# The first half of an output projection moved into the SSD chunks, on x rows kept on chip, with decay rows read by broadcast

## The chip, the cores and the metric

The kernel runs on one core of one Trainium2 chip. The metric is the device time of one execution, in microseconds (us), median of three runs. The engines are TensorE (PE, with its weight loads PEld), VectorE (DVE), ScalarE (ACT), GpSimd (POOL) and the DMA queues, which SyncE (SP) and GpSimd feed. Each engine runs its own stream of instructions in order; streams meet at semaphores.

## What is computed

Two transformer-like blocks, sequence 1024, width 1024, float32. The change is in the second one:

```python
h = rmsnorm_2(x, norm1_w); p = h @ w_in
y_ssd = ssd_mixer(...)     # Mamba-2, 8 chunks of 128 tokens, 16 heads of 64, 2 groups, state 128
y_ml  = mlstm_mixer(...)   # 8 heads of 128
x = x + concat([y_ssd, y_ml]) @ w_out          # (1024 x 2048) @ (2048 x 1024)
x = x + hier_moe(rmsnorm_2(x, norm2_w)); return rmsnorm_2(x, norm_f_w)

# one SSD chunk, per head
a_cs = cumsum(dt*a);  L = exp(a_cs[l] - a_cs[s]) for s <= l, else 0
y = (C B^T * L) @ (dt*x) + (C @ state) * exp(a_cs)
state = state * exp(a_cs[-1]) + B^T @ (exp(a_cs[-1]-a_cs) * dt*x)
y = group_rmsnorm((y + D*x) * silu(z)) * norm_w
```

## The kernel before

The program is a row of stages, each a block that all engines leave together. In the second block they are `projections`, `ssd_chunks`, `mlstm_chunks` and `second_block`, then the routed experts.

**Products in high and low halves.** Every large product takes three float32r products (`mm3`, L343 to L345): high x high, high x low, low x high. Each operand is split into a high half (ACT copy to float32r) and a low half (DVE subtraction). `h_hl` (called `hl` in the code) is the one big buffer with both halves of a 1024 x 1024 activation.

**`ssd_chunks`** loops over 8 chunks. The carried state binds them: chunk k+1's `inter` product (C times state, L1758) needs chunk k's new state. Per chunk, PE does: `inter`; `intra` (16 small products of the masked matrix `sd_l` with dt*x, L1767); `state` (L1773); then `front(k+1)`, which makes the sums over the chunk (L1720), C B^T (L1722), turns x and B (L1727, L1731) and builds the exponents of L for 16 heads in PSUM: four broadcast products of `adt` with a triangle (L1737) and one of the identity with a matrix of -1e30 (L1739) for each four heads, in a PSUM pair `sd_psA` that they share with the transposes; last `result(k)`, which turns y (L1747). ACT copies x, squares y, takes the root, and takes the 16 exponentials of `sd_l` (L1613) in two halves (`decay`), the first before and the second after the root. DVE adds and scales y, carries the state (L1680, L1683), makes dt*x and its decayed copy (L1648, L1650), multiplies `sd_l` by C B^T (L1656) and writes the turned y times its gain to `sd_yt` (L1702). GpSimd only makes D*x (L1564); ahead of the loop its queue writes 15 blocks of zeros to `scratch_ys` (L1558). The turned y goes to DRAM (`scratch_y_ssd`, L1539).

**`second_block`** has three stages after `mlstm_chunks`, which leaves its own result in `h_hl`: `add_product` "w1" (`h_hl` times the lower half of w_out, added to x rows that a DMA brings, L799), `load_split` "ys" (y_ssd read back and split into `h_hl`), and `add_product` "w2" with the upper half of w_out and the following norm ("n4"). An `add_product` loads 16 weight tiles of 128x512 (L791), splits them (ACT L809, DVE L823), and runs 16 sums of 24 products.

## Time and profile before

| | us |
|---|---|
| median of 3 runs (3782.6 to 3791.38) | 3783.6 |
| the profiled execution | 3789.3 |
| its span | 3787.6 |
| stage `ssd_chunks`, 2401.6 to 2581.2 | 179.6 |
| stage `mlstm_chunks`, 2581.2 to 2825.4 | 244.2 |
| stage "w1", 2825.4 to 2931.9 | 106.5 |
| stage "ys", 2931.9 to 2949.5 | 17.6 |
| stage "w2" with its norm, 2949.5 to 3062.5 | 113.0 |

The times of the stages are positions in the profiled execution, counted from the start of its span. The profiled execution is 0.15% above the median of the runs. A busy share of an engine is that of the whole stage; what a stage costs is read from its ends, since no engine works across them.

### The profile page before, as it was taken

Reading aid. Unit: us, or ns where it says so; the run is one execution under the profiler, and the core shown is the slowest. Engines: PE = TensorE matmul, PEld = TensorE weight load, DVE = VectorE, ACT = ScalarE, POOL = GpSimd, SP = SyncE. Lnnn points to the kernel's source line nnn. Section 1 sums busy time; section 2 is a strip of 40 time slices with the busy share of each in tenths; the row PEclk is TensorE's granted clock in tenths of the full one; section 3 lists DMA queues with packets and bytes.
Section 4 is the critical chain, followed back from the end, with each engine's and each line's share of the span. In section 5 each row is a group of like instructions: output and inputs, shape, how many; then the busy total and the mean of one; then the engine's idle time right before and its main releaser. Section 6 shows DMA issues by size and latency. Waiting matters only on the chain. (4 is left out here: it accounts for less than half of the span.)

```text
span 3787.6 us, 40241 instructions
## 1 busy us (share of the span) xinstructions
PE 3401.2 (90%) x15444; PEld 2779.5 (73%) x15444; DVE 1902.0 (50%) x2156; ACT 1371.0 (36%) x1950; POOL 217.9 (6%) x309
## 2 busy tenths in 40 slices
PE   6999999898899999996999999787969759999994
PEld 5888888686788888885887788666857647777773
DVE  3444433433344554446206553473431468888885
ACT  4322333212311111113312322343550327878783
POOL 0000000000000000000010000210000110000002
PEclk8999999998999999998999999896769879999997
DMA  3122221432111111112232223422121329999996
GB/s 96 62 73 91 66 76 58 161 111 100 45 50 50 50 38 45 50 39 72 98 83 67 95 95 106 167 78 95 67 82 43 114 97 362 393 386 391 388 387 235
DMA packets 325203, 489.17 MB, mean 129 GB/s; under 512 B 58848, under 2 KB 223200, under 8 KB 324064
## 3 DMA queue, kind: packets, MB, share of 16 engines
q1 hardware_dynamic: 292496, 372.25, 28.8%
q0 software_dynamic: 27984, 98.58, 6.9%
q10 hardware_dynamic: 4608, 16.78, 1.1%
q8 instruction: 75, 1.23, 0.1%
q14 instruction: 40, 0.33, 0.0%
HBM read 402.08 MB, written 85.46 MB: 129 GB/s over the span
## 5 line engine op out<-in xcount | busy, mean ns | idle before, releaser
L947 DVE TENSOR_TENSOR x_rows<-x_rows,ff_psd 128x512 f32<-128x512 f32 x352 | 239.5, 688 | 333.8 <-PE ff_psd L345 333.8
L343 PE MATMUL m_ps<-h_hl,m_w_hl 128*128 128x512 f32 x896 | 356.0, 397 | 11.6 <-DVE m_w_hl L530 11.6
L344 PE MATMUL m_ps<-h_hl,m_w_hl 128*128 128x512 f32 x896 | 349.4, 390 | 0.0
L345 PE MATMUL m_ps<-h_hl,m_w_hl 128*128 128x512 f32 x896 | 349.4, 390 | 0.0
L2415 DVE TENSOR_TENSOR h_hl<-ex_stage,h_hl 128x1024 fp32r<-128x1024 f32 x256 | 304.8, 1221 | 39.5 <-ACT h_hl L2411 38.2
L2411 ACT ACTIVATE h_hl<-ex_stage 128x1024 fp32r<-128x1024 f32 x256 | 269.1, 1058 | 81.2 <-DMA ex_stage<-in_exp_w_up_dram 46.6
L343 PE MATMUL pj_turned<-h_hl,pc_w_hl 128*128 128x512 f32 x576 | 224.9, 390 | 6.2 <-DVE pc_w_hl L1290 6.2
L344 PE MATMUL pj_turned<-h_hl,pc_w_hl 128*128 128x512 f32 x576 | 224.2, 389 | 0.0
L345 PE MATMUL pj_turned<-h_hl,pc_w_hl 128*128 128x512 f32 x576 | 224.1, 389 | 0.0
L343 PEld LDWEIGHTS m_ps<-h_hl,m_w_hl 128*128 128x128 f32 x896 | 168.6, 188 | 50.5 <-DVE m_w_hl L530 12.0
L927 ACT ACTIVATE ff_act_hl<-ff_act 128x1024 fp32r<-128x1024 f32 x22 | 23.3, 1060 | 485.4 <-DVE ff_act L965 485.4
L344 PEld LDWEIGHTS m_ps<-h_hl,m_w_hl 128*128 128x128 f32 x896 | 168.6, 188 | 38.6 <-issue 3.8
L345 PEld LDWEIGHTS m_ps<-h_hl,m_w_hl 128*128 128x128 f32 x896 | 168.5, 188 | 35.2
L2415 DVE TENSOR_TENSOR ex_w_hl<-ex_stage,ex_w_hl 128x1024 fp32r<-128x1024 f32 x128 | 154.0, 1222 | 47.6 <-ACT ex_w_hl L2411 46.6
L530 DVE TENSOR_TENSOR m_w_hl<-m_stage,m_w_hl 128x1024 fp32r<-128x1024 f32 x56 | 68.5, 1223 | 193.6 <-ACT m_w_hl L458 193.6
L343 PE MATMUL ff_psg<-h_hl,ff_wg 128*128 128x512 f32 x352 | 139.5, 396 | 22.3 <-DVE ff_wg L938 11.3
L2411 ACT ACTIVATE ex_w_hl<-ex_stage 128x1024 fp32r<-128x1024 f32 x128 | 133.0, 1056 | 56.3 <-DMA ex_stage<-in_exp_w_gate_dram 47.2
L343 PE MATMUL ff_psd<-ff_wd,ff_act_hl 128*128 128x512 f32 x352 | 137.7, 391 | 4.3 <-DVE ff_act_hl L967 4.3
L343 PE MATMUL w_ps<-w_w_hl,h_hl 128*128 128x512 f32 x256 | 105.7, 413 | 39.2 <-DVE w_w_hl L823 39.2
L344 PE MATMUL ff_psd<-ff_wd,ff_act_hl 128*128 128x512 f32 x352 | 137.6, 391 | 0.0
L344 PE MATMUL ff_psg<-h_hl,ff_wg 128*128 128x512 f32 x352 | 137.6, 391 | 0.0
L345 PE MATMUL ff_psg<-h_hl,ff_wg 128*128 128x512 f32 x352 | 137.5, 391 | 0.0
(498 smaller groups left out, 7751.3 us busy)
## 6 DMA issues: line engine op xcount, KB each, us to landing
ex_stage<-in_exp_w_gate_dram SPq DMA_DIRECT2D x128, 512.0 KB, 5.4
ex_stage<-in_exp_w_up_dram SPq DMA_DIRECT2D x128, 512.0 KB, 7.6
ex_stage<-in_exp_w_down_dram SPq DMA_DIRECT2D x128, 512.0 KB, 6.3
m_stage<-in_w_in_dram SPq DMA_DIRECT2D x56, 512.0 KB, 4.1
...
```

Source lines behind the costliest of these rows:

```text
L343: nc.tensor.matmul(out, w_hl[0], x_hl[0], start=first, stop=False)
L344: nc.tensor.matmul(out, w_hl[0], x_hl[1], start=False, stop=False)
L345: return nc.tensor.matmul(out, w_hl[1], x_hl[0], start=False, stop=last)
L530: v.tensor_tensor(w_hl[s][:, 1], stage[:, s], f32(w_hl[s][:, 0]), ALU.subtract).then_inc(s_lo, 1)
L927: nc.scalar.activation(a_hl[b][:, 0], act_f[:], ACT.Copy).then_inc(s_ah, 1)
L947: v.tensor_tensor(dst, dst, ps_d[g % NB][:], ALU.add).then_inc(s_add, 1)
L2411: nc.scalar.activation(w_hl[u][:, 0], stage[:, s], ACT.Copy).then_inc(s_hi, 1)
L2415: nc.vector.tensor_tensor(w_hl[u][:, 1], stage[:, slot(e, u)], f32(w_hl[u][:, 0]), ALU.subtract).then_inc(s_lo, 1)
```

## The change

One. `ssd_chunks` no longer builds the exponents of L on PE. The running sums of `adt` are made once, as 16 rows, by PE and DVE in `projections` and stored to a new DRAM tensor `scratch_cum`. In `ssd_chunks` a DMA reads the 16 rows of a chunk into all 128 partitions (`sd_cum_l`, 1 MB, one buffer). GpSimd adds the mask (`causal`, a 128x2048 addition) into `sd_l`, which now has two buffers. ACT takes the exponentials from there. Sums over chunks are made once for all 8 chunks, ahead of the loop.

Two. C B^T is copied to SBUF (`sd_cb`, new `c_by_b`), and the product with `sd_l` reads it there. The decay of the state moves from DVE to GpSimd.

Three. The 15 stores of zeros move to the end of `projections`, on SP's queue, from a 128x128 tile.

Four. The x rows (`x_rows3`, 4 MB) are loaded at the start of `ssd_chunks` and stay. The upper half of w_out is loaded and split there into `h_hl`, which is free until `mlstm_chunks`: eight tiles ahead of the loop, eight in its first pass (`w_high`, `w_low`). The turned y of a chunk is split (`sd_y_hl`), and `out_product(k-1)`, 48 products of 128x512, stands between `front(k+1)` and `result(k)` on PE. DVE adds it to the x rows (`add`).

Five. The store of y, the stage "ys" and one of the two `add_product` stages are gone. The one that is left keeps the norm and loads no x rows.

```diff
@@ projections, engine SP, behind the loads of the column weights
+            sp.wait_ge(s_zero, 1)
+            for x in range(scr.NX):
+                row = (scr.NT - 2 * T + x) * P
+                sp.dma_start(scr.ys[row:row + P, :].rearrange("p (a n) -> p a n", n=P),
+                             zero[:].unsqueeze(1).to_broadcast([P, KT, P])).then_inc(s_zst, 16)
+            sp.wait_ge(s_zst, 16 * scr.NX)
...
@@ projections, engine PE
+                elif f == 9:
+                    pe.wait_ge(s_up, 2)
+                    pe.wait_ge(s_rows, 1)
+                    for k in range(T):
+                        last = nc.tensor.matmul(ps_cum[:, k * P:(k + 1) * P], scr.adt[:, k], upper[:], start=True, stop=True)
+                    last.then_inc(s_pcum, 1)
...
@@ ssd_chunks, engine SP
                 sp.dma_start(xbc[:, k % 2], scr.xbc[k]).then_inc(s_xbc[k % 2], 16)
+                if k >= 1:
+                    sp.wait_ge(g_l, k)
+                sp.dma_start(cum_l[:].rearrange("p h n -> p (h n)"),
+                             scr.cum[k].rearrange("(a h) n -> a (h n)", a=1).broadcast_to([P, H * P])).then_inc(s_cum, 16)
...
             chunk_loads(1)
-            for k in range(NC):
-                if k + 2 < NC:
-                    chunk_loads(k + 2)
-                sp.wait_ge(d_yt, 2 * k + 2)
-                sp.dma_start(scr.y_ssd[:, :, k * P:(k + 1) * P].rearrange("f p s -> p f s"), yt[:]).then_inc(s_st, 16)
-            sp.wait_ge(s_st, 16 * NC)
+            for n in range(NW):
+                h, k = divmod(n, XT)
+                wait(sp, s_wlo, n - NS + 1)
+                sp.dma_start(stage[:, n % NS], w_v[:, k, h * HALF:(h + 1) * HALF]).then_inc(s_w[n % NS], 16)
+            for k in range(2, NC):
+                chunk_loads(k)
@@ ssd_chunks, engine POOL
+            pool.dma_start(x_tm[:], scr.x4.rearrange("(t p) d -> p t d", p=P)).then_inc(s_x, 16)
+
+            def causal(k):
+                pool.wait_ge(s_cum, 16 * (k + 1))
+                wait(pool, p_in, k - 1)
+                nc.gpsimd.tensor_tensor(lt[:, k % 2], cum_l[:], neg[:].unsqueeze(1).to_broadcast([P, H, P]),
+                                        ALU.add).then_inc(g_l, 1)
...
             for k in range(NC):
-                pool.wait_ge(a_A, 6 * k + 2)
                 if k:
-                    pool.wait_ge(d_y, k)
-                nc.gpsimd.tensor_tensor(heads(xd[:]), heads(x_r[:]), per_head(d_row[:]), ALU.mult).then_inc(g_x, 1)
-            pool.wait_ge(s_zst, 16 * scr.NX)
+                    pool.wait_ge(p_inter, k)
+                    pool.wait_ge(d_st, k)
+                    nc.gpsimd.tensor_tensor(heads(state[:]), heads(state[:]), per_head(e3[:, 2, k]), ALU.mult).then_inc(g_st, 1)
+                if k + 1 < NC:
+                    skip(k + 1)
+                if k + 2 < NC:
+                    causal(k + 2)
@@ ssd_chunks, engine ACT
+            def decay(k, g):
+                act.wait_ge(g_l, k + 1)
+                for h in range(g * HG, (g + 1) * HG):
+                    last = nc.scalar.activation(lt[:, k % 2, h], lt[:, k % 2, h], ACT.Exp, bias=ncum[:, k, h:h + 1])
+                last.then_inc(a_l, 1)
...
+            decay(0, 0)
+            decay(0, 1)
+            for n in range(XT):
+                w_high(n)
             for k in range(NC):
                 if k + 1 < NC:
                     front(k + 1)
+                    decay(k + 1, 0)
                 act.wait_ge(d_y, k + 1)
...
                 if k + 1 < NC:
-                    decay(k + 1, (2, 3))
+                    decay(k + 1, 1)
+                if k == 0:
+                    for n in range(XT, NW):
+                        w_high(n)
+                act.wait_ge(d_yt, 2 * k + 2)
+                wait(act, p_w2, 2 * k)
+                nc.scalar.activation(yh[:, 0], yt[:], ACT.Copy).then_inc(a_yh, 1)
@@ ssd_chunks, engine PE
+            def out_product(k):
+                pe.wait_ge(d_yl, k + 1)
+                for h in range(2):
+                    cut = slice(h * HALF, (h + 1) * HALF)
+                    if k == 0:
+                        pe.wait_ge(s_wlo, XT * (h + 1))
+                    wait(pe, d_add, 2 * (k - 1) + h + 1)
+                    for t in range(XT):
+                        last = mm3(nc, psD[:, h], (yh[:, 0, t], yh[:, 1, t]), (hl[:, 0, t, cut], hl[:, 1, t, cut]),
+                                   t == 0, t == XT - 1)
+                    last.then_inc(p_w2, 1)
...
                 if k + 1 < NC:
                     front(k + 1)
+                    c_times_b(k + 1)
+                if k:
+                    out_product(k - 1)
                 result(k)
+            out_product(NC - 1)
@@ program
-            x_tm = second_block(nc, A, scr.x4, scr, hl, ctx)
-            routed_experts(nc, A, scr, hl)
+        recycle_semaphores(nc)
+        add_product(nc, "w1", x_tm, hl, A.w_out_2[0].rearrange("(k p) n -> p k n", p=P)[:, KT:],
+                    norm=("n4", A.norm2_w_2[0], dict(rows_out=scr.h)))
+        recycle_semaphores(nc)
+        routed_experts(nc, A, scr, hl)
```

The change writes the streams in another order. Three places show it; line numbers of the changed kernel differ from those before.

PE, one pass of the loop before, from the `state` product of one chunk to the `intra` products of the next:

```order
L1773 MATMUL sd_psC<-sd_xdec,sd_b 128x512 x2
L1720 MATMUL sd_psD<-adt,sd_upper 128x16
...
L1722 MATMUL sd_psD<-sd_xbc 128x128 x2
L1727 MATMUL sd_psA<-sd_ident,sd_xbc 128x128 x8
L1731 MATMUL sd_psE<-sd_ident,sd_xbc 128x128 x2
L1737 MATMUL sd_psA<-sd_upper,adt 128x128 x4
L1739 MATMUL sd_psA<-sd_neg,sd_ident_r 128x512
...
L1747 MATMUL sd_psA<-sd_ident,sd_y 128x128 x8
L1758 MATMUL sd_psC<-sd_state,sd_xbc 128x512 x2
L1767 MATMUL sd_psB<-sd_xdt,sd_l 128x64 x16
```

The same pass after (the rows of `mm3` stand 16 times each):

```order
L1854 MATMUL sd_psC<-sd_xdec,sd_b 128x512 x2
L1794 MATMUL sd_psA<-sd_ident,sd_xbc 128x128 x8
L1799 MATMUL sd_psA<-sd_ident,sd_xbc 128x128 x2
L1806 MATMUL sd_psB<-sd_xbc 128x128 x2
L343 MATMUL sd_psD<-h_hl,sd_y_hl 128x512
L344 MATMUL sd_psD<-h_hl,sd_y_hl 128x512
L345 MATMUL sd_psD<-h_hl,sd_y_hl 128x512
...
L1827 MATMUL sd_psA<-sd_ident,sd_y 128x128 x8
L1841 MATMUL sd_psC<-sd_state,sd_xbc 128x512 x2
L1847 MATMUL sd_psB<-sd_xdt,sd_l 128x64 x16
```

The 16 products and 4 mask products of the decay have left this place and the 48 products of the output have come in, ahead of the transposes of y.

DVE, one pass after, from the addition of the `intra` products on:

```order
L1731 TENSOR_TENSOR sd_y<-sd_y,sd_psB 128x1024
L1737 TENSOR_TENSOR sd_y<-sd_y,sd_xd 128x1024
L1739 TENSOR_TENSOR sd_y<-sd_y,sd_z 128x1024
L1743 TENSOR_TENSOR sd_state<-sd_state,sd_psC 128x1024
L1686 TENSOR_TENSOR sd_xdt<-sd_x,dt 128x1024
L1689 TENSOR_TENSOR sd_xdec<-sd_xdt,sd_e 128x1024
...
L1699 TENSOR_TENSOR sd_l<-sd_l,sd_cb 128x1024
L1713 TENSOR_TENSOR x_rows<-x_rows,sd_psD 128x512 x2
L1767 TENSOR_TENSOR sd_yt<-sd_psA,sd_norm 128x512 x2
L1770 TENSOR_TENSOR sd_y_hl<-sd_yt,sd_y_hl 128x1024
L1728 TENSOR_TENSOR sd_y<-sd_psC,sd_e 128x1024
```

Against before, the state's decay (L1680) is gone from it, and the copy of C B^T, two additions to the x rows and the low half of the turned y have come in, the additions ahead of `sd_yt`.

GpSimd, the end of its constants and its loop before:

```order
L1546 MEMSET sd_ones 128x128
L1547 MEMSET sd_eps 128x1
L1548 MEMSET sd_after 128x128
L1551 AFFINE_SELECT sd_after<-sd_after 128x128
L1554 MEMSET sd_zero 128x1024
L1558 DMA scratch_ys<-sd_zero 128x1024 x15
L1564 TENSOR_TENSOR sd_xd<-sd_x,sd_d 128x1024 x8
```

The same place after, to the first pass of the loop with a state to decay:

```order
L1594 DMA x_rows<-scratch_x 128x8x1024
L1599 TENSOR_TENSOR sd_l<-sd_cum_l,sd_neg 128x2048
L1605 TENSOR_TENSOR sd_xd<-sd_x,sd_d 128x1024
L1599 TENSOR_TENSOR sd_l<-sd_cum_l,sd_neg 128x2048
L1605 TENSOR_TENSOR sd_xd<-sd_x,sd_d 128x1024
L1599 TENSOR_TENSOR sd_l<-sd_cum_l,sd_neg 128x2048
L1616 TENSOR_TENSOR sd_state<-sd_state,sd_e 128x1024
```

Where GpSimd had one operation of 1024 columns a chunk it has two of them and one of 2048.

## Rows read from the trace of the kernel before

**Rows 1.** The page's first line.

```profile
span 3787.6 us, 40241 instructions
```

**Rows 2.** Busy time of each engine by stage, with the granted clock.

```profile
core 0: us, PE busy (x) PEld busy (x) DVE busy (x) ACT busy (x) POOL busy (x), PEclk, DMA share, GB/s
2825.40:2931.90 106.50, 96.14 (x384) 74.77 (x384) 21.59 (x32) 9.88 (x16) 0.96 (x1) 0.89 0.22 79
2931.90:2949.50 17.60, 0.00 (x0) 0.00 (x0) 9.82 (x9) 8.45 (x8) 0.00 (x0) 0.57 0.69 238
2949.50:3062.50 113.00, 99.08 (x448) 80.35 (x448) 48.83 (x55) 39.03 (x56) 19.84 (x11) 0.94 0.23 80
2401.60:2581.20 179.60, 136.86 (x828) 107.39 (x828) 117.28 (x118) 81.30 (x229) 28.60 (x34) 0.88 0.37 126
2581.20:2825.40 244.20, 200.46 (x1138) 185.17 (x1138) 85.47 (x189) 128.74 (x429) 16.57 (x26) 0.66 0.19 70
```

**Rows 3.** Timeline: the first instructions of the stages "w1" and "w2".

```profile
2825.44 9.02 SPq L791 DMA_DIRECT2D w_stage<-in_w_out_dram  x7
...
2949.53 9.65 SPq L791 DMA_DIRECT2D w_stage<-in_w_out_dram  x10
```

**Rows 4.** Who waits for whom, 2420 to 2575: total, times, longest.

```profile
PE sd_psA L1747 <- ACT sd_l L1613: 20.9, 14, 2.7
```

**Rows 5.** Timeline of one chunk: start, us, engine, line [idle before].

```profile
2504.89 1.22 DVE L1670 TENSOR_TENSOR sd_y<-sd_y,sd_psB 128x1024 f32<-128x1024 f32 x1 [2.36 <-PE sd_psB L1767]
...
2507.51 1.04 PE L1727 MATMUL sd_psA<-sd_ident,sd_xbc 128*128 128x128 f32 x8
...
2509.31 2.22 POOL L1564 TENSOR_TENSOR sd_xd<-sd_x,sd_d 128x1024 f32<-128x1024 f32 x1 [18.52 <-ACT sd_x L1599]
...
2509.80 1.22 DVE L1683 TENSOR_TENSOR sd_state<-sd_state,sd_psC 128x1024 f32<-128x1024 f32 x1
...
2510.94 1.67 DVE L1648 TENSOR_TENSOR sd_xdt<-sd_x,dt 128x1024 f32<-128x1024 f32 x1
...
2515.71 2.18 ACT L1613 ACTIVATE sd_l<-sd_psA,sd_neg_c 128x128 f32<-128x128 f32 x8
...
2518.85 3.10 PE L1758 MATMUL sd_psC<-sd_state,sd_xbc 128*128 128x512 f32 x4
...
2521.78 3.68 PE L1767 MATMUL sd_psB<-sd_xdt,sd_l 128*128 128x64 f32 x32
...
2525.30 1.94 PE L1773 MATMUL sd_psC<-sd_xdec,sd_b 128*128 128x512 f32 x4
...
2525.57 1.22 DVE L1670 TENSOR_TENSOR sd_y<-sd_y,sd_psB 128x1024 f32<-128x1024 f32 x1 [2.36 <-PE sd_psB L1767]
```

**Rows 6.** GpSimd's operation by tile: ns min/median/max, first and last start.

```profile
L1564 POOL TENSOR_TENSOR sd_xd<-sd_x,sd_d x8: 1896/2224/2598, 2413.1 to 2550.6; 128x1024 f32<-128x1024 f32 x8
```

**Rows 7.** As rows 2, five microseconds around an `inter` product.

```profile
2455.00:2460.00 5.00, 4.68 (x16) 2.46 (x15) 2.78 (x4) 0.67 (x3) 0.00 (x0) 0.66 0.19 53
```

**Rows 8.** Timeline of stage "w1": an addition for 24 products of 128x512.

```profile
2931.23 0.69 DVE L831 TENSOR_TENSOR x_rows<-x_rows,w_ps 128x512 f32<-128x512 f32 x1 [4.75 <-PE w_ps L345]
```

**Rows 9.** Timeline of `ssd_chunks`: first `intra` product, second chunk's addition of them.

```profile
2418.08 3.76 PE L1767 MATMUL sd_psB<-sd_xdt,sd_l 128*128 128x64 f32 x32 [0.85 <-DVE sd_l L1656]
...
2442.67 1.22 DVE L1670 TENSOR_TENSOR sd_y<-sd_y,sd_psB 128x1024 f32<-128x1024 f32 x1 [2.77 <-PE sd_psB L1767]
```

**Rows 10.** Weight tiles in stages "w1" and "w2", landing time of the x rows.

```profile
2841.66 0.63 ACT L809 ACTIVATE w_w_hl<-w_stage 128x512 fp32r<-128x512 f32 x1 [1.45 <-DMA w_stage<-in_w_out_dram]
...
2964.29 1.27 ACT L809 ACTIVATE w_w_hl<-w_stage 128x512 fp32r<-128x512 f32 x2 [1.06 <-DMA w_stage<-in_w_out_dram]
...
DMA to landing us min/median/max: 19.8/19.8/19.8
```

**Rows 11.** End of `projections`: column-weight loads; SP's queue, 2300 to 2402.

```profile
L1149 SPq DMA_DIRECT2D pc_stage<-in_w_in_dram x34: 367/368/678, 1981.5 to 2354.6; - x34
...
q1 hardware_dynamic: 6240, 3.15, 10.8%
```

402 lines of the change are left out of this document (199 added, 203 removed).

## The prediction

> **What bounds the kernel now.** I read the page first: the span is 3787.6 us [rows 1], against 3789.3 for the whole profiled execution and a median of 3783.6. Then one table by stage. The stages share nothing, so the change can be priced at three places: what goes, what `ssd_chunks` becomes, and what `projections` gets on top. `ssd_chunks` lasts 179.6 us and PE is busy 136.9 of them; "w1" lasts 106.5, "ys" 17.6 [rows 2]. Third I read the timeline of a chunk and the chain of waits. In a chunk nothing is saturated. The period is 20.68 us, from one addition of the `intra` products to the next (2504.89 to 2525.57) [rows 5]. It is a loop of short steps over three engines: y on DVE, square and root on ACT, the second half of the exponentials (2.18 us), the product with C B^T, the transposes, `inter`, `intra`, y again. The reader should see that PE stands still ahead of the transposes because `sd_psA` is held by exponents that ACT has not read: 20.9 us in 14 waits [rows 4]. Just behind that gap `inter` takes 3.10 us where `state`, four instructions of the same size, takes 1.94 [rows 5]; the granted clock of those five microseconds is 0.66 of 2.4 GHz, a mix of both levels [rows 7].
>
> **What goes.** From the first load of "w1" to the first load of "w2" are 2949.53 - 2825.44 = 124.1 us [rows 3]. The stage that is left is "w2" as it stood: same loads, products and norm, nothing else at its start. So **-124.1**, a difference of two positions and not an estimate. The store of y went with it.
>
> **What `projections` gets.** PE is the bound there, so its 8 products of 128 columns go on top: `state` does 8 pieces of 128 columns in 1.94 us [rows 5], so +1.9. The 15 stores of zeros (7.86 MB) start when the last column weights have been asked for, at 2354.6, and the stage ends at 2401.6. Loads in pieces of 512 bytes on SP's queue moved 3.15 MB in 10.8% of 102 us, 286 GB/s [rows 11]; 7.86 MB at that rate are 27.5 us, over at about 2382. I take 0. Cover gone (half the rate) it would end at 2410 and cost 8.
>
> **What a chunk becomes, on PE.** `inter` at full clock 1.94 (as `state`), `intra` 3.68, `state` 1.94. Ten transposes, two products for C B^T and eight transposes of y are 20 pieces of 0.13 (1.04 for eight) = 2.6, and 0.4 for ACT to empty `sd_psA` [rows 5]. The output product: in "w1" 24 products take 4.75 + 0.69 = 5.44 us [rows 8], so 48 take 10.9. Sum **21.4 us**, nearly without a gap, where a chunk had a period of 20.68. The decay's products are out of it, and so is the wait of rows 4, because ACT now reads SBUF.
>
> **On DVE.** Seven operations of 1024 columns from SBUF alone (add D*x, times z, dt*x, its decayed copy, two products with C B^T, low half of y), three from PSUM (the two y steps, state), each 1.22 [rows 5]: 12.2. The scale of y with the reciprocal about 1.0 (my estimate from half the columns), copy of C B^T 0.35, two additions to the x rows 2 x 0.69 [rows 8], `sd_yt` two halves 1.4 by the same row. Sum 16.3.
>
> **On GpSimd, and what it blocks.** `sd_xd` takes 1.90 at its shortest [rows 6]. One decay of state and one D*x are 3.8, the mask of 2048 columns by proportion another 3.8: 7.6 us a chunk against 1.9. Rows 5 show what this does to DVE. `sd_xd` runs from 2509.31 to 2511.53. `sd_xdt`, which reads SBUF only, starts at 2510.94 and takes 1.67 instead of 1.22, ending 1.08 behind GpSimd's end. `sd_state` with `sd_psC` starts at 2509.80, in the middle of it, and takes its usual 1.22. So an operation with a PSUM operand runs beside GpSimd, one from SBUF alone waits for its end. In the new order D*x falls where dt*x would start (both wait for the same x), and the mask falls on its decayed copy; the state's decay falls on the low half of y, ahead of the next y. The first two, 1.9 + 3.8 = 5.7, lie in a stretch in which DVE has no PSUM work of its own, so DVE and its blocked time come to 16.3 + 5.7 = **22.0 us**. The third is taken out of time in which DVE waits for PE anyway.
>
> The Trainium skill, "SBUF — State Buffer", section "SBUF: two separate sides", calls the pair of ports that DVE and GpSimd share an exclusive lock: whoever starts first keeps it for its whole instruction. By that rule the change, which quadruples GpSimd's work and moves the operand `cbt` from PSUM to SBUF, costs DVE up to 7.6 us a chunk and not 5.7; by the trace's own rows the sum stands as above.
>
> **The period.** Two loops of 21.4 and 22.0 us that hand to each other: y on DVE must be done before PE's C B^T, PE's output product before DVE's additions. With about 1 us for the handovers I take **23 us**. Bounds: below 20.7 (all of it hidden), above 22.0 + 1.9 + 2 more handovers, 26.
>
> ACT has 2.2 + 2.2 for exponentials, 1.1 for x, 0.4 for B, 1.7 for squares, 0.3 for the root, two table loads of 1.3 and 1.1 for the high half: under 12 by the busy time of its old loop (81.3 / 8 = 10.2 [rows 2]). It bounds nothing.
>
> **Start and end of the stage.** The first `intra` starts at 2418.1 and the second chunk's y addition ends at 2443.9 [rows 9]. Now DVE must write eight low halves of weights ahead of the first y. The tiles queue behind 1 MB of sums, z and x, and GpSimd's queue brings 4 MB of x rows, which took 19.8 us to land in "w1" [rows 10]; the second 1 MB waits for the first mask. I put the first tile at 2425. Tiles then come every 1.16 us (2.33 for two, "w2") or 2.08 (beside the x rows, "w1") [rows 10]: eighth at 2436, with 2442 as the other end. Then y 4.8 us, squares, root and the second half of exponentials 6.8, product 1.2, eight more tiles 8.5, `sd_yt`, high and low half and first step of y 4.8, addition 1.2: 2463, **19 later**. Add C B^T, the first output product with its first microseconds at half clock (13) and the transposes: pass 1 ends at 2478. Six more periods less the last pass's `front` (3): 2478 + 138 - 3 = 2613. Then the last turned y is split (4.6 with PE still), multiplied (13, again from the low clock) and added (1): 2631.6. `mlstm_chunks` started at 2581.2, so **+50.4**.
>
> **Sum.** -124.1 + 50.4 + 1.9 = -71.8. Against its own 3789.3 that is 3717.5, and against the median, which is 5.7 lower, **3712**.
>
> **The rivals.**
>
> *Port bound* (0.22). Every one of GpSimd's 7.6 us stands in DVE's way, and the loop has 16.3 + 7.6 = 23.9 and 1.5 of handovers: period 25.4, +2.4 x 6 = +14, 3726. For it: rows 5 as read above. Against: the state's decay starts while DVE waits for the transposes.
>
> *Slow start* (0.10). Tiles at 2.08 and late sums for chunk 2, whose load stands behind all 16 tiles on SP's queue: +16, 3728.
>
> *All hidden* (0.15). Period 20.7, set as now by the loop of steps, now without the wait of rows 4: -2.3 x 6 = -14, 3698. Against: PE alone has 21.4.
>
> *Does not do what it says* (0.07). The output product runs in sequence with the chunk's loop, because the transposes of y or the next `inter` stand behind it on PE and everything waits for them: 20.68 + 10.9 = 31.6, +8.6 x 6 = +52, 3764. Still faster, because "w1" and "ys" are gone.
>
> *Slower* (0.04). PE runs the chunk at 1.2 GHz. In `mlstm_chunks` PE is busy 82% of the time and the granted clock is 0.66 [rows 2]; so a busy PE of small products with short gaps is no safeguard. All but `intra` double: (21.4 - 3.7) x 2 + 3.7 = 39.1, +16.1 x 6 = +97, and about 12 at start and end: 3821. It decides from a period of 35 on, where 12 x 6 eats the 72. Against: half of a chunk's PE time is now dense products like those of "w1", whose stage shows 0.89 with its start included [rows 2]. The Trainium skill, "TensorE: Matmul & The Clock Gate", section "What's actually happening", has the throttled state as the default that activity lifts; rows 7 agree, since the low clock is seen right behind the gap.
>
> My own forecast gets 0.42. It is the likeliest; neither start nor port has to go wrong.
>
> **How the numbers follow.** A change of 0.3%, 11 us, is about what a measurement of this kernel can tell from none. Forecast 3712; "all hidden" with a start of bare 1.16 pace gives 3690, port and start together 3742, and period 26 with the slow start 3746. 3690 to 3750 leaves out the sequential case and the slow clock, 0.11, and some of the edges. Faster: all but the slow clock and some tail of the sequential case, 0.94; same 0.02; slower 0.04.
>
> **What the profile would show.** Right: the `mm3` of `sd_psD` 0.226 us apart in the chunks; clock at 1.0 from the third chunk on; additions of `intra` 23 us apart; `sd_xdt` and `sd_xdec` at 2 to 4 us; mlSTM starting near 2634; the stage "w1" as long as "w2" was, 113 us; zeros landed ahead of the last store of `projections`. Wrong: a period of 26 or more (then see whether PE or DVE waits, and for whom), the mask of 2048 taking over 5 us, an `inter` at 3.1 us in each chunk, DVE still waiting for weight tiles behind 2442, or `ssd_chunks` starting later than 2405.

## The result, and the profile after

| | before | after | forecast |
|---|---|---|---|
| median of 4 runs | 3783.1 (3780.8 to 3791.4) | 3724.4 (3721.9 to 3727.0) | 3712 (3690 to 3750) |
| span of the profiled execution | 3787.6 | 3725.2 | -71.8 |
| ahead of `ssd_chunks` | 2401.6 | 2407.7 | +1.9, was +6.1 |
| stage `ssd_chunks` | 179.6 | 237.6 | +50.4, was +58.0 |
| stage `mlstm_chunks` | 244.2 | 245.0 | 0, was +0.8 |
| stages "w1" and "ys" | 124.1 | 0 | -124.1 |
| the product and norm that are left, and the experts | 838.1 | 834.9 | 0, was -3.2 |

The ratio of after to before is 0.984, 95% interval 0.9826 to 0.9853: faster by 1.6%. In medians the change is -58.7 us. In spans it is -62.4 against the forecast -71.8: the stage and what stands ahead of it are 7.6 and 4.2 us above the forecast, `mlstm_chunks` 0.8, and the last row is 3.2 below. The last two are within what one profile differs from the next: the same changed kernel, profiled again (e10), has its experts 9.5 us longer than here (726.7 against 717.2 from their first load to the end).

The changed kernel's busy time by stage, to be read against [rows 2] (span of the stretch, busy time and count of each engine, granted clock, DMA share, GB/s): `ssd_chunks`, `mlstm_chunks`, then the one output stage that is left.

```profile
2407.70:2645.30 237.60, 186.16 (x882) 142.34 (x882) 175.13 (x159) 101.87 (x234) 74.92 (x34) 0.86 0.31 115
2645.30:2890.30 245.00, 203.37 (x1138) 187.93 (x1138) 85.50 (x189) 128.81 (x429) 16.58 (x27) 0.66 0.19 69
2890.30:3005.30 115.00, 98.78 (x448) 80.53 (x448) 48.38 (x55) 38.77 (x56) 19.83 (x11) 0.93 0.23 78
```

**The start of the stage.** Timeline of `ssd_chunks` from its first load at 2407.71; compare [rows 9]. The bracket is the idle time before, and what ended it.

```profile
2409.05 0.66 SPq L1566 DMA_DIRECT2D sd_d<-in_ssd_d_dram  x1
2409.75 0.45 SPq L1568 DMA_DIRECT2D sd_norm<-in_ssd_norm_w_dram  x1
...
2414.70 4.49 POOL L1599 TENSOR_TENSOR sd_l<-sd_cum_l,sd_neg 128x2048 f32<-128x2048 f32 x1 [4.32 <-ACT sd_x L1631]
...
2427.88 1.23 DVE L1686 TENSOR_TENSOR sd_xdt<-sd_x,dt 128x1024 f32<-128x1024 f32 x1 [25.26 <-DMA sd_norm<-in_ssd_norm_w_dram]
...
2433.68 3.65 PE L1847 MATMUL sd_psB<-sd_xdt,sd_l 128*128 128x64 f32 x16 [18.19 <-DVE sd_l L1699]
2434.60 2.62 ACT L1646 ACTIVATE h_hl<-w_stage 128x512 fp32r<-128x512 f32 x4 [10.53 <-DMA w_stage<-in_w_out_dram]
```

And the DMA issues of the same stretch (KB of one, median us from issue to landing):

```profile
sd_cum_l<-scratch_cum SPq DMA_DIRECT2D x4, 1024.0 KB, 8.3
x_rows<-scratch_x POOLq DMA_DIRECT2D x1, 4096.0 KB, 18.2
...
sd_d<-in_ssd_d_dram SPq DMA_DIRECT2D x1, 8.0 KB, 11.2
sd_norm<-in_ssd_norm_w_dram SPq DMA_DIRECT2D x1, 4.0 KB, 18.1
```

DVE begins dt*x only at 2427.88, though its x was there at about 2414.7. It waits for one semaphore that counts two loads of 8 and 4 KB. They now stand behind the first chunk's three loads on SP's queue and land after 11.2 and 18.1 us. So `intra` starts 26.0 us after the stage's first load, where it had been 16.5.

**A chunk.** Timeline of the changed kernel, one period; compare [rows 5].

```profile
2501.92 1.90 POOL L1605 TENSOR_TENSOR sd_xd<-sd_x,sd_d 128x1024 f32<-128x1024 f32 x1 [6.13 <-DVE sd_y L1739]
...
2502.82 2.08 DVE L1686 TENSOR_TENSOR sd_xdt<-sd_x,dt 128x1024 f32<-128x1024 f32 x1
...
2506.53 1.23 DVE L1699 TENSOR_TENSOR sd_l<-sd_l,sd_cb 128x1024 f32<-128x1024 f32 x1
2506.79 5.46 POOL L1599 TENSOR_TENSOR sd_l<-sd_cum_l,sd_neg 128x2048 f32<-128x2048 f32 x1 [2.97 <-DMA sd_cum_l<-scratch_cum]
...
2507.87 5.06 DVE L1755 TENSOR_SCALAR sd_y<-sd_y,sd_rstd 128x512 f32<-128x512 f32 x2
...
2513.15 1.03 PE L1827 MATMUL sd_psA<-sd_ident,sd_y 128*128 128x128 f32 x8
...
2514.03 1.88 PE L1841 MATMUL sd_psC<-sd_state,sd_xbc 128*128 128x512 f32 x4
2515.18 1.28 DVE L1767 TENSOR_TENSOR sd_yt<-sd_psA,sd_norm 128x512 f32<-128x512 f32 x2
2515.74 3.68 PE L1847 MATMUL sd_psB<-sd_xdt,sd_l 128*128 128x64 f32 x32
...
2515.99 1.90 POOL L1616 TENSOR_TENSOR sd_state<-sd_state,sd_e 128x1024 f32<-128x1024 f32 x1 [3.74 <-PE sd_psC L1841]
2516.49 1.06 ACT L1676 ACTIVATE sd_y_hl<-sd_yt 128x1024 fp32r<-128x1024 f32 x1 [5.45 <-DVE sd_yt L1767]
2517.58 1.39 DVE L1770 TENSOR_TENSOR sd_y_hl<-sd_yt,sd_y_hl 128x1024 fp32r<-128x1024 f32 x1 [1.12 <-ACT sd_y_hl L1676]
2518.89 1.21 DVE L1728 TENSOR_TENSOR sd_y<-sd_psC,sd_e 128x1024 f32<-128x1024 f32 x1
...
2520.16 1.98 PE L1854 MATMUL sd_psC<-sd_xdec,sd_b 128*128 128x512 f32 x4 [0.73 <-DVE sd_y L1728]
```

GpSimd's decay of the state (L1616) follows PE's `inter` and ends at 2517.89. DVE's low half of the turned y (L1770) begins at 2517.58 and ends 1.08 us behind it, at 2518.97; the scaling and `state` come behind that.

The scaling of y (L1728) starts at 2496.79 and 2518.89: the period is 22.1, and 22.11 on average over the next ones. It is 23.82 in the last two, where PE's `state` takes 3.68 us in place of 1.98, the length it has at half clock:

```profile
2564.39 3.68 PE L1854 MATMUL sd_psC<-sd_xdec,sd_b 128*128 128x512 f32 x4 [0.74 <-DVE sd_y L1728]
```

Both loops look full in a period. Busy time as in the first fence, over 22 us from 2498 on:

```profile
2498.00:2520.00 22.00, 21.04 (x110) 16.48 (x110) 20.67 (x18) 11.41 (x27) 9.26 (x3) 1.00 0.27 108
```

PE is busy 21.04 and DVE 20.67 of 22.0 us. Which one sets it, and whether the mask that holds DVE for 4 us costs anything, can't be read from busy shares. That was the question for the experiments.

### The profile page after: what moved, and what is told of

It is laid out like the page before. It is cut to its first block and busy times, and to the rows that moved or that the text cites. A ratio compares the mean times of both kernels' runs of the same rounds, so it can differ in the third digit from the quotient of the medians.

```text
span 3725.2 us, 39593 instructions
## 1 busy us (share of the span) xinstructions
PE 3361.8 (90%) x15130; PEld 2747.4 (74%) x15130; DVE 1930.8 (52%) x2158; ACT 1374.0 (37%) x1931; POOL 263.9 (7%) x312
## 5 line engine op out<-in xcount | busy, mean ns | idle before, releaser
L343 PE MATMUL ff_psg<-h_hl,ff_wg 128*128 128x512 f32 x352 | 139.9, 397 | 21.6 <-PE ff_psd L345 10.9
L343 PE MATMUL ff_psd<-ff_wd,ff_act_hl 128*128 128x512 f32 x352 | 138.2, 393 | 4.3 <-DVE ff_act_hl L967 4.3
L344 PE MATMUL ff_psd<-ff_wd,ff_act_hl 128*128 128x512 f32 x352 | 138.0, 392 | 0.0
L345 PE MATMUL ff_psd<-ff_wd,ff_act_hl 128*128 128x512 f32 x352 | 137.8, 391 | 0.0
```

Source lines behind the costliest of these rows:

```text
L343: nc.tensor.matmul(out, w_hl[0], x_hl[0], start=first, stop=False)
L344: nc.tensor.matmul(out, w_hl[0], x_hl[1], start=False, stop=False)
L345: return nc.tensor.matmul(out, w_hl[1], x_hl[0], start=False, stop=last)
```

## The experiments

All kernels start from the changed one. "Stage" is from SP's first load of `ssd_chunks` to ACT's first instruction in `mlstm_chunks`, 239.9 us in the changed kernel (2.3 more than in the table above, where it ends with the first instruction of any engine). "y(0)" is the start of the first chunk's y, "scaling" that of the second chunk's L1728, both after the first load; "periods" are the six from there on. The median is that of 4 or 5 runs (none for e4, which leaves out seven eighths of the output product in the chunks, so that only the stage is compared), the ratio is to the kernel before on the same chip.

| kernel | y(0) | scaling | periods | stage | median | ratio, 95% |
|---|---|---|---|---|---|---|
| changed kernel | 39.0 | 63.5 | 25.6, 22.1 x3, 23.8 x2 | 239.9 | 3724.4 | 0.984 (0.9826 to 0.9853) |
| e1_small_first | 35.8 | 60.5 | 25.5, 22.1 x5 | 233.4 | 3725.6 | 0.9837 (0.9818 to 0.9856) |
| e2_scale_tt | 39.6 | 65.8 | 25.8, 22.5 x3, 23.8 x2 | 243.5 | 3731.7 | 0.985 (0.9832 to 0.9868) |
| e3_low_later | 39.8 | 63.0 | 28.4, 23.0, 22.4, 22.2 x2, 20.6 | 240.0 | 3727.2 | 0.9841 (0.9826 to 0.9856) |
| e4_one_eighth | 39.3 | 64.2 | 25.0, 23.7, 23.8, 23.9, 24.1, 22.3 | 227.6 | | |
| e5_affine | 37.1 | 63.0 | 24.0, 23.8 x2, 22.1 x3 | 234.7 | 3721.7 | 0.9842 (0.9822 to 0.9861) |
| e6_relu | 37.5 | 68.8 | 24.4, 22.1 x5 | 240.2 | 3731.3 | 0.9863 (0.9843 to 0.9883) |
| e7_relu_late_small | 36.6 | 58.4 | 23.1, 21.2 x5 | 226.6 | 3712.3 | 0.9817 (0.9797 to 0.9837) |
| e8_start | 39.8 | 64.4 | 25.4, 22.1 x5 | 236.6 | 3724.5 | 0.9845 (0.9827 to 0.9863) |
| e9_together | 25.5 | 51.4 | 21.4, 21.2 x5 | 216.8 | 3701.7 | 0.9783 (0.977 to 0.9796) |
| e10_again | 39.0 | 65.6 | 25.4, 22.1 x5 | 236.8 | 3726.7 | 0.9847 (0.9833 to 0.986) |
| e11_tail | 26.1 | 52.7 | 21.1, 21.2 x5 | 213.4 | 3702.6 | 0.9777 (0.9759 to 0.9796) |
| e12_spread | 26.5 | 53.9 | 21.6, 21.2 x5 | 215.1 | 3690.7 | 0.9747 (0.9724 to 0.977) |

A stage of one profile tells 1 us; a median of whole runs does not tell 5, as e1's shows. So the small effects are read from positions in the traces, and only e9, e11 and e12 stand clear of the changed kernel as whole runs. The interval of e7 reaches up to 0.9837, above the lower ends of the changed kernel's two (0.9826 and 0.9833), though its four runs lie below each run of e5, e6 and e8 on the same chip.

### e1_small_first

```diff
-            chunk_loads(0)
             sp.dma_start(d_row[:], ...)
             sp.dma_start(norm[:], ...)
+            chunk_loads(0)
```

> The two small loads (sd_d, sd_norm) are issued ahead of the first chunk's three loads; nothing else differs from the changed kernel. Theory (the first products waited for these two loads: DVE's sd_xdt stood 25.26 us until 2427.9 and landed behind 10 MB of other loads): both land within some 3 us, sd_xdt starts right behind the first x copies at about 2414.7, the first intra at 2420 to 2425 instead of 2433.7 (26.0 after the stage's start becomes 13 to 18), and the stage gets shorter by 4 to 9 us, to 229 to 234; the total is then about 3716 to 3720. Rival A (weight tiles bind the first pass: their loads land from 2434.6 on at full DMA rate, and the first y addition and the second eight tiles come no earlier): the first intra is early, but the second chunk's y addition stays at 64 to 66 us after the start, and the stage stays at 237 +- 1. Rival B (the first exponentials bind, they start at 2419.3 behind the 4.5 us mask and the last ends at 2424.1): the first intra is at 21 to 23 after the start at the earliest, the gain not above 5 us.

Both loads landed in 2.4 and 2.5 us; DVE began dt*x as soon as x was there, 8.8 after the first load, and the first `intra` came at 18.4 instead of 26.0. Of these 7.5 us only 3.2 reached y(0), and 3.0 the second scaling: the weight tiles bind next, as rival A had it, though not in full. The timeline of this kernel:

```profile
2413.92 1.22 DVE L1686 TENSOR_TENSOR sd_xdt<-sd_x,dt 128x1024 f32<-128x1024 f32 x1 [13.90 <-ACT sd_x L1631]
...
2423.56 7.06 PE L1847 MATMUL sd_psB<-sd_xdt,sd_l 128*128 128x64 f32 x32 [9.04 <-DVE sd_l L1699]
...
2432.68 2.57 ACT L1646 ACTIVATE h_hl<-w_stage 128x512 fp32r<-128x512 f32 x4 [8.30 <-DMA w_stage<-in_w_out_dram]
```

The stage is 6.5 shorter; the other 3.4 are two periods of 23.8 that are 22.1 here. So the late small loads are worth 3 us by themselves, read from one profile; the median, 3725.6, does not show them.

### e2_scale_tt

```diff
-v.tensor_scalar(y[:, cut], y[:, cut], rstd[:, g:g + 1], None, ALU.mult)
+v.tensor_tensor(y[:, cut], y[:, cut], rstd[:, g:g + 1].to_broadcast([P, GW]), ALU.mult)
```

> The two normalizing products of a chunk (DVE tensor_scalar, 5.06 us together while GpSimd's mask runs) are written as tensor_tensor with a broadcast operand; values are the same. Theory (the single-input form is held until GpSimd's instruction ends, the two-input form is not): the pair takes 1.2 to 1.4 us, and the second half of the sd_l product comes 3.7 us earlier. Price of the block, by the theory that PE sets the period (DVE then only waits longer for the sum of the output product, 2514.0, and still stands 0.7 us ahead of PE's state product): the period stays at 22.1, the stage at 237 +- 1. Rival (DVE sets the period, as the prediction had it, 22.0 busy): the period falls by 1 to 3 us to 19.5 to 21.3, and the stage by 6 to 20. Second rival (the two-input form is blocked too, as sd_xdt beside sd_xd with 2.08 against 1.22): the pair takes 3 to 5 us and nothing changes.

The second rival held: the form with two SBUF inputs is held as well, to the end of GpSimd's instruction.

```profile
2554.78 5.07 POOL L1599 TENSOR_TENSOR sd_l<-sd_cum_l,sd_neg 128x2048 f32<-128x2048 f32 x1 [3.35 <-DMA sd_cum_l<-scratch_cum]
...
2555.48 5.52 DVE L1755 TENSOR_TENSOR sd_y<-sd_y,sd_rstd 128x512 f32<-128x512 f32 x2
```

The pair takes 5.52 instead of 5.06, and the period 22.46 instead of 22.11. It did not take the block away, but it shows where the block stands. In the changed kernel the pair ends at 2512.93 and PE's transposes of y begin at 2513.15, right behind the output product. Here it ends at 2561.00 and they begin at 2561.06, about 0.3 us later behind that product than there. A block any longer is paid for.

### e3_low_later

```diff
 v.tensor_tensor(heads(y[:]), heads(y[:]), both(psB), ALU.add).then_inc(d_yb, 1)
+y_low(k - 1)      # waits for ACT's high half, then the low half
 ...
-dve.wait_ge(a_yh, k + 1)
-v.tensor_tensor(yh[:, 1], yt[:], f32(yh[:, 0]), ALU.subtract).then_inc(d_yl, 1)
```

> DVE makes the low half of the turned y (1.39 us, ahead of it 1.12 us of waiting for ACT's high half) behind the scaling and the addition of the next chunk's y instead of ahead of them. Theory (PE sets the period but stands 0.73 to 0.87 us in each for DVE's scaling that frees the state product's PSUM): the scaling starts 2.5 us earlier, PE's wait for it goes, the period falls by 0.7 to 0.9 to 21.2 to 21.4, and the stage by 4 to 7 us over seven periods. With the wait gone the half clock of the last three state products (3.68 instead of 1.98) may go as well: then 2 to 5 us more. Rival (the wait moves on: DVE was at 95 per cent, state addition, dt*x and C by B come 1.4 us later and the squares and root with them, so that PE waits for the normalized y at the end of the chunk): the period stays at 22.1 +- 0.3, with a new wait of PE for DVE ahead of result.

The rival held where there is a mask, the theory where there is none. PE's wait for the scaling went, but DVE's work slid back so that the mask fell on the first `sd_l` product, and PE stood 0.80 us for the normalized y:

```profile
2555.38 4.66 POOL L1599 TENSOR_TENSOR sd_l<-sd_cum_l,sd_neg 128x2048 f32<-128x2048 f32 x1 [2.16 <-DMA sd_cum_l<-scratch_cum]
...
2555.93 5.20 DVE L1699 TENSOR_TENSOR sd_l<-sd_l,sd_cb 128x1024 f32<-128x1024 f32 x1
...
2562.18 1.09 PE L1831 MATMUL sd_psA<-sd_ident,sd_y 128*128 128x128 f32 x8 [0.80 <-DVE sd_y L1760]
```

And the scaling, which reads PSUM, runs in the middle of GpSimd's decay of the state. In the changed kernel the low half stands in that place and is held by it:

```profile
2565.07 1.90 POOL L1616 TENSOR_TENSOR sd_state<-sd_state,sd_e 128x1024 f32<-128x1024 f32 x1 [5.03 <-PE sd_psC L1845]
2565.57 1.22 DVE L1732 TENSOR_TENSOR sd_y<-sd_psC,sd_e 128x1024 f32<-128x1024 f32 x1
```

The last period has no mask. There the `sd_l` product takes 1.23, and `intra` starts 21.2 us after the one before (2587.03, 2608.20): PE's own work.

### e4_one_eighth

```diff
-for t in range(XT):
-    last = mm3(nc, psD[:, h], (yh[:, 0, t], yh[:, 1, t]), ..., t == 0, t == XT - 1)
+last = mm3(nc, psD[:, h], (yh[:, 0, 0], yh[:, 1, 0]), ..., True, True)
```

> The output product in the chunks sums only one of its eight 128-row parts (6 instead of 48 products a chunk), so the SSD half of the output is incomplete and the routing behind it differs: only the stage ssd_chunks is compared. PE loses 42 products of 0.233, 9.8 us, in each period; DVE keeps all. Theory (PE sets the period at 22.1, DVE with its block is right behind it, at 20.3 busy): the period falls only to 20.3 to 21, and PE stands 8 us a period for DVE. Rival A (DVE's chain is far from binding, its block is cover): 13 to 17 us. Rival B (GpSimd or the loads bind): the period is set by waits for the mask or the rows of cum, 17 to 20. The first pass and the start do not move by more than 1 us by any of them.

None of the three: the period got longer, 23.8, with 9.8 us of PE's work gone. The timeline of this kernel:

```profile
2533.56 4.69 POOL L1599 TENSOR_TENSOR sd_l<-sd_cum_l,sd_neg 128x2048 f32<-128x2048 f32 x1 [3.60 <-DMA sd_cum_l<-scratch_cum]
...
2534.00 4.93 DVE L1755 TENSOR_SCALAR sd_y<-sd_y,sd_rstd 128x512 f32<-128x512 f32 x2
...
2538.99 1.97 PE L1825 MATMUL sd_psA<-sd_ident,sd_y 128*128 128x128 f32 x8 [9.66 <-DVE sd_y L1755]
...
2540.75 3.62 PE L1839 MATMUL sd_psC<-sd_state,sd_xbc 128*128 128x512 f32 x4
```

PE now stands 9.66 us for the normalized y, so the mask's block lies bare on the path; and behind that gap PE runs at half clock (transposes 1.97 for 1.03, `inter` 3.62 for 1.88). The output product thus cost the loop nothing by itself: it filled a gap that the other chain leaves anyway, and kept the clock up. That chain (DVE with the block, and PE at half clock at its end) is 23.8 without it. At full clock `inter` and the transposes would be 2.7 shorter. But DVE stands only 2.08 us for the `intra` products there, so that its own steps would take over at about 21.8 (an estimate from these rows and that wait), above PE's own 21.2.

### e5_affine and e6_relu: the mask shorter, and gone

```diff
 # e5
-nc.gpsimd.tensor_tensor(lt[:, k % 2], cum_l[:], neg[...].to_broadcast([P, H, P]), ALU.add)
+nc.gpsimd.affine_select(out=lt[:, k % 2], in_=cum_l[:], compare_op=ALU.is_ge, fill=-1e30,
+                        base=0, pattern=[[0, H], [1, P]], channel_multiplier=-1)
 # e6
+for h in range(H):   # ACT, for chunk k+2, where it waits for the turned y
+    nc.scalar.activation(lt[:, k % 2, h], cum_l[:, h], ACT.Relu, scale=-1.0, bias=cum_c[:, k, h:h + 1])
+nc.scalar.activation(m, m, ACT.Exp, scale=-1.0)              # 1024 columns, twice
-v.tensor_copy(cbm[:], cbt)
+v.tensor_tensor(cbm[:], cbt, upper[...].to_broadcast([P, G, P]), ALU.mult)
```

> GpSimd makes the masked rows by one instruction with one input (affine_select, 128x2048, the causal condition from the indices) in place of the addition of sd_neg; same values. The runs so far show that DVE's instruction that reads only SBUF stands until GpSimd's ends (both forms: 5.06 and 5.52 us for the normalizing pair, 5.20 for the sd_l product), and that with the output product cut to an eighth the period is longer, not shorter: DVE's chain, with the block, its 1.12 us of waiting for ACT and the 0.4 us gaps, sets the period of 22.1. Theory (what GpSimd spends on the mask comes off DVE's chain one for one until PE, at 20.6 in the one period without a mask, binds): 128x128 of this form takes 0.29 us in the start of the stage; at the rate of the addition (2.2 ns a column) it stays 4.5 and nothing changes; at 1.1 to 1.5 ns it takes 2.2 to 3.0 and the period falls by 1.3 to 1.5, to 20.6 to 20.9, the stage by 8 to 11 us. Rival (PE sets the period anyway): 22.1 whatever the mask takes.

> No mask on GpSimd: ACT takes the differences by 16 Relu (of minus the row plus the cumulated sum, so never above zero once its sign is turned) for chunk k+2 while it would wait for the turned y (5.5 to 5.9 us a chunk), then two exponentials of 1024 columns with scale -1 in place of 16 of 128; the causal mask goes into DVE's copy of C by B, now a product with sd_upper. Same values within rounding. GpSimd keeps 3.8 us a chunk, ACT gets 4.9 more and 2.7 less of its 11.4. Theory (the mask's block on DVE sets the period): the normalizing pair takes 0.88, the period falls to 20.6 to 21.0 (PE's own work, as in the one period of the third experiment that had no mask), the stage by 8 to 12 us. Rival A (PE sets 22.1 already): no change, PE's waits stay. Rival B (ACT becomes late: Relu and the exponential want two tables of functions, or the squares come late): new waits of DVE for ACT, period 22 to 25.

In both the period stayed at 22.11, as the rival said, but not by the rival's reason: it is not PE's work that sets it. The mask took 2.0 to 2.8 us in e5 and was gone in e6, and the normalizing pair fell from 5.06 to 2.43 and 0.89. From the timeline of e5:

```profile
2552.88 2.53 POOL L1599 TENSOR_SCALAR_AFFINE_SELECT sd_l<-sd_cum_l 128x2048 f32<-128x2048 f32 x1 [3.27 <-DMA sd_cum_l<-scratch_cum]
...
2553.66 2.43 DVE L1755 TENSOR_SCALAR sd_y<-sd_y,sd_rstd 128x512 f32<-128x512 f32 x2
```

From the timeline of e6:

```profile
2503.05 1.98 PE L1854 MATMUL sd_psC<-sd_xdec,sd_b 128*128 128x512 f32 x4 [0.73 <-DVE sd_y L1728]
...
2512.87 0.89 DVE L1755 TENSOR_SCALAR sd_y<-sd_y,sd_rstd 128x512 f32<-128x512 f32 x2
...
2521.00 1.90 POOL L1608 TENSOR_TENSOR sd_state<-sd_state,sd_e 128x1024 f32<-128x1024 f32 x1 [12.18 <-PE sd_psC L1841]
2521.37 2.61 DVE L1770 TENSOR_TENSOR sd_y_hl<-sd_yt,sd_y_hl 128x1024 fp32r<-128x1024 f32 x1 [1.12 <-ACT sd_y_hl L1676]
```

PE's wait for the scaling is the same 0.73 with the mask, with half of it and without. The last two rows say why. The low half, which reads only SBUF, takes 2.61 us in place of 1.22: it stands until GpSimd's decay of the state is done (2522.90) and ends 1.08 behind it, as in the changed kernel. The decay itself waits for PE's `inter`. So from `inter` on, decay, low half, scaling and `state` follow each other at fixed distances, whatever the mask does. In e5 and e6 the low half takes 2.6 us in each of the six periods. Without that hold the one above would end 1.39 earlier, more than PE's wait; that is worked out from these rows, and no run moved the decay alone.

In the changed kernel two chains thus have nearly one length. In the one just told the decay holds the low half for the last 0.17 us of its 1.39; DVE's own steps, with the mask's block of 4 us and 1.12 us of waiting for ACT, are the other. Shortening the mask leaves the first. e6 is no gain in all: in the first pass its 16 Relu stand ahead of ACT's high half, for which DVE waits 7.56 us, and the second scaling is 5.3 late.

### e7_relu_late_small

> The edits of e6_relu, e3_low_later and e1_small_first together. Theory (two chains of nearly one length, DVE's with the block and PE's with its 0.73 us wait for DVE's scaling; each alone hides the other): with both loosened the period is PE's work alone, 20.3 to 20.7, and with the early start the stage is 15 to 20 us shorter than in the changed kernel, about 220 to 225; total about 3705. Rival (one of the two edits has all of it): as e6 plus 6.5 us for the start.

The theory of two chains held, and its period but for 0.5 us. With the low half behind the scaling, the decay of the state holds nothing that PE waits for (the scaling reads PSUM); with the mask gone, DVE's own steps are short enough. The period falls by 0.95 to 21.16, which neither edit gave alone. The stage is 13.3 shorter, not 15 to 20: the last part, from the last scaling on, grew by 2.4, as the low half now stands late there too.

### e8_start

```diff
+# small loads first; four weight tiles ahead of chunk_loads(1)
-pool.dma_start(x_tm[:], ...)       # ahead of causal(0)
+pool.dma_start(x_tm[:], ...)       # behind causal(1)
```

> The changed kernel with its first pass rearranged: the two small loads first, four weight tiles ahead of the second chunk's loads, the load of the x rows (4 MB, 10 us of all DMA engines at 400 GB/s) behind GpSimd's second mask; the loop is untouched. Theory (with the small loads early, the first pass is bound by the weight tiles, which land behind x rows and the second chunk: y(0) at 35.8 us after the start although the first intra ended at 25.5): y(0) at 26 to 28, the second chunk's scaling at 50 to 54 instead of 60.5 (63.5 in the changed kernel), the stage 9 to 13 us shorter than in the changed kernel, total about 3713. Rival (the second chunk's own loads, mask and exponentials bind, now later in the queue): scaling at 58 to 61, no more than the 3 us of e1_small_first.

Theory and rival both fell: y(0) at 39.8, the second scaling at 64.4. The timeline shows why:

```profile
2416.52 4.50 POOL L1599 TENSOR_TENSOR sd_l<-sd_cum_l,sd_neg 128x2048 f32<-128x2048 f32 x1 [6.92 <-DMA sd_cum_l<-scratch_cum]
2416.68 5.42 DVE L1687 TENSOR_TENSOR sd_xdt<-sd_x,dt 128x1024 f32<-128x1024 f32 x1 [13.99 <-ACT sd_x L1632]
...
2425.31 6.69 DVE L1700 TENSOR_TENSOR sd_l<-sd_l,sd_cb 128x1024 f32<-128x1024 f32 x2
...
2430.86 0.93 POOL L1612 DMA_DIRECT2D x_rows<-scratch_x  x1
...
2432.63 29.59 SPq L1574 DMA_DIRECT2D w_stage<-in_w_out_dram  x12
```

Here the mask's block does cost: dt*x and the `sd_l` products take 5.42 and 6.69 (1.2 and 2.4 alone), DVE frees the first tile slot at 2432.6, and the fifth tile queues behind 4 MB of x rows after all.

### e9_together and e10_again

```diff
 # e9 = e5 + e3 + e1, and in the first pass
+for n in range(NS): w_high(n)     # ACT, ahead of decay(0, ...)
+for n in range(NS): w_low(n)      # DVE, ahead of matrices(0, ...)
+# eight tiles asked for ahead of chunk_loads(1), x rows behind the second mask
```

> The edits of e5_affine (mask by affine_select, 2.5 us instead of 4.7 to 5.5), e3_low_later and e1_small_first, and the first pass in another order: weight tiles 0 to 3 are loaded behind the first chunk, ACT and DVE split them before the exponentials and the sd_l products (in e8_start DVE came to them only behind 5.4 us each in dt*x and in the sd_l product, blocked by the masks, so that tile 4 was asked for behind the 4 MB of x rows), tiles 4 to 7 are asked for ahead of the second chunk's loads, the x rows behind the second mask. Theory: y(0) at 20 to 24 us after the start (39.0 in the changed kernel, 35.8 with the small loads first), the second chunk's scaling at 45 to 50 (63.5), periods 21.2 from the third chunk on (22.11), no half clock in the loop; stage 210 to 216 against 239.9, total 3697 to 3702. Rival A (the second chunk's loads, 2.3 MB behind the tiles, bind its front, mask and exponentials): scaling at 54 to 58, total about 3708. Rival B (the shorter mask still blocks the sd_l product in each chunk, where the low half stands later): periods 21.9 to 22.2.

> The changed kernel itself once more, beside the one above. Theory (the half clock of the state product is no property of a chunk but comes and goes: it stood in periods 6 and 7 of the changed kernel's profile, in 2, 3 and 4 of e5_affine's, in none of e1's, e6's and e8's, always with PE's 0.73 us wait ahead of it): some number of periods, not again the same ones, last 23.82, the others 22.11. Rival (it is fixed by the program): again periods 6 and 7 alone.

Side by side on one chip e9 took 3701.7 and the changed kernel 3726.7; the intervals of their ratios do not touch. y(0) came at 25.5 (2 to 5 later than expected), the scaling at 51.4, between theory and rival A; the periods at 21.17; the stage 216.8, just above the theory. Rival B fell: the `sd_l` product does take up to 2.6 us beside the mask, but that is now covered. In e10 all periods behind the first were 22.1: the half clock in `state` is not fixed by the program. I don't know what brings it. Seven profiles have PE's 0.73 us wait ahead of `state` (those of the changed kernel, e1, e2, e5, e6, e8 and e10), 42 times in all, and `state` ran at half clock behind 9 of them: the last three chunks of the changed kernel and of e2, two in e5, and the last chunk of e1. It did so behind none in e6, e8 and e10, and in no later chunk of the kernels without that wait.

### e11_tail and e12_spread

```diff
 # e11, last pass on PE                      # e12, projections
-out_product(NC - 2)                         -if f == 9: 8 products of the sums
-result(NC - 1)                              +if f == 9: 4 of them
+out_product(NC - 2, (0,))                   +if f == 10: transposes, then 4 of them
+result(NC - 1)
+out_product(NC - 2, (1,))
```

> e9_together with another end: in the last pass PE turns the last chunk's normalized y between the two halves of the output product of the chunk before it, and the last high and low halves have a buffer of their own (that of the decay rows, free by then). Before, PE stands from the last turn of y to its low half with nothing to do (3.6 us) and starts the last output product at half clock. Theory: yt, high and low half (1.3, 1.1, 1.2 us) lie beside 5.5 us of product, PE does not stand and its clock does not fall: from the last scaling to the next stage 31 to 34 us instead of 38.2, the stage 210 to 213 instead of 216.8, total about 3697. Rival (the normalized y is late: it is ready only where the whole product of the chunk before ends, so PE waits for it between the halves): 36 to 38, no change.

> e11_tail with the eight products for the running sums in projections (1.92 us in one piece) in two pieces of four, the second behind the transposes one column later. In each profile of a kernel with them the granted clock falls to 0.83 to 0.93 in one stretch of 10 us behind them and to 0.90 to 1.00 in the next, and stays 1.00 in the kernel before. Theory (the narrow products themselves cost 1.9 us, the clock's fall the other 1.6): without the fall projections get 1 to 2 us shorter, the products stay 1.9 together. Rival (the fall has nothing to do with how many stand together, or four narrow products behind the transposes make it fall twice): 0 or 1 to 2 us longer. Nothing else moves.

e11: from the last scaling to the next stage 33.8 instead of 38.2, clock 1.00 to the end; the stage is 3.4 shorter. The medians of e9 and e11 don't tell that apart. e12: the rival held, the clock still fell, as the busy time by stretch shows. The kernel before:

```profile
2120.00:2130.00 10.00, 10.00 (x68) 8.35 (x67) 6.13 (x6) 2.92 (x3) 0.89 (x1) 1.00 0.22 73
```

The changed kernel:

```profile
2120.00:2130.00 10.00, 10.00 (x63) 8.22 (x62) 3.93 (x4) 2.92 (x3) 0.89 (x1) 0.88 0.32 105
```

e12:

```profile
2120.00:2130.00 10.00, 10.00 (x65) 8.05 (x64) 6.03 (x6) 2.91 (x3) 0.89 (x1) 0.83 0.22 78
```

What stands right ahead of the fall is something else. Two more stretches of the changed kernel:

```profile
2114.00:2127.00 13.00, 13.00 (x81) 10.82 (x80) 5.85 (x6) 4.38 (x6) 0.89 (x1) 1.00 0.26 83
...
2128.00:2129.00 1.00, 1.00 (x3) 0.77 (x3) 0.96 (x2) 0.00 (x0) 0.05 (x1) 0.50 0.33 135
```

The eight products end there at about 2113.8, and the clock stays 1.00 up to 2127. It falls within 1 us of the end of 32 products of 8x8 columns (`gv_ident`, 2124.8 to 2127.0). The kernel before has the same 32, with no fall, and not the eight ahead of them. So the two together are what the runs show; the 32 alone don't do it, and the eight alone were not tried. e12 kept both.

Its median is the lowest, but its five runs lie between 3676.6 and 3703.3, and the profiled one is the slowest of them; what made the others faster is not shown.

## Why the prediction was right, and where it was not

**What goes, -124.1.** As forecast. The stage that is left was forecast as long as "w2"; from its first weight load to the next stage's first load it is 117.7 us against 115.5. The experts behind it came out 5.4 shorter. No edit touches either; over the profiles of the other kernels but e4 the first lies between 115.1 and 117.3, the second between 717.4 and 726.7.

**The period, 23.** Measured 23.26 on average over the six, and that it came so near is luck: two of its steps were wrong and made up for each other. PE's 21.4 was right: 21.2 where nothing else holds it (e3's last period, e7, e9). DVE's sum of 22.0 was not: 20.67 busy in 22.0 us. The mask was mis-sized (3.8 by proportion; 4.49 alone, and 5.46 where DVE's `sd_l` product was still running for the first 0.97 of it), and it fell on the normalizing pair, not on the decayed copy. The Trainium skill, "GPSIMD Engine Reference", section "Elementwise — side-by-side cycle accounting", gives 4.50 for an addition of 2048 columns; the first mask, 4.49, agrees.

The step that failed is "the third is taken out of time in which DVE waits for PE anyway". The decay of the state falls on the low half of y as forecast, but DVE does not wait for PE there (its only wait is 1.12 us for ACT), and PE waits for DVE: `inter`, decay, held low half, scaling, `state`. This chain gives PE its 0.73 us wait and a period of 22.11, which is 0.95 longer than PE's own work. DVE's steps with the mask's block are no more than 0.2 us behind it, which is why the mask could go without a gain. The "1 us for handovers" was a guess, and it has the size of this difference. The rest of the 23.26 is the first of the six periods, 25.6 with eight weight tiles in it, and 1.7 each for two `state` products at half clock.

**What GpSimd blocks.** The mechanism held in each trace: an operation that reads SBUF alone waits for GpSimd's end, whether it has one SBUF input or two (5.06, 5.52, 5.20, 5.42 us), one with a PSUM operand does not (the scaling in e3 takes 1.22 in the middle of the decay of state). The Trainium skill, "SBUF — State Buffer", section "SBUF: two separate sides", says so of operations with two SBUF inputs, and of others only in a two-port performance mode. The trace agrees on the first; in which mode the one-input scaling ran, no row here shows. The step that failed is the one from blocked time to period. The rival "port bound" was right that the state's decay stands in DVE's way too, but took the sum of DVE's time for the period, 25.4: the mask's part of it is hidden.

**Start.** The prediction counted the first y from the weight tiles alone, 34.4 us after the stage's start; it came at 39.0. It put the first tile at 23.4, where its split began at 26.9, and did not follow two small loads past the three large ones on SP's queue, which moved the first `intra` from 16.5 to 26.0. The Trainium skill, "DMA: Bandwidth & Descriptors", section "Queues, rings and completion order", has each queue's descriptors consumed in order on every engine; the landing times, 2.4 and 2.5 us ahead of the large loads and 11.2 and 18.1 behind them, agree. The second chunk's y addition ended at 66.0 after the stage's start (61.4 forecast). Of these 4.6 us the small loads are 3 (e1); the late tiles are the rest.

**End.** From the last addition to the next stage 32.1 against 30.6, with the half clock where it was expected.

**`projections`, +1.9.** The products took the forecast 1.92. Missed: the clock behind them, 0.88 and 0.95 in two stretches of 10 us, 1.7 us. A fall of this size stands in all thirteen profiles with these products, and not in the one before. Another 2.3 stood there before `projections`, whose first PE work is at 1779.1 against 1776.8. No edit touches that part, and it is at 1776.4 in e1 and at 1779.9 in e6, so it is scatter between profiles. The zeros were hidden as forecast, 10 us ahead of the last store, though they landed at about 2393 and not at 2382.

The other rivals: "all hidden" fell with PE's 21.2, the output product in sequence with the period of 22.1 in place of 31.6, and the slower clock with the 1.00 in most chunks, though e4 shows how near the low clock is once the dense products are away. Three of the prediction's own signs of being wrong did show: a mask over 5 us, DVE still waiting for weight tiles behind 2442, and `ssd_chunks` starting later than 2405.
